# First norm of a two-block transformer kernel: squares summed in advance, root applied before the modulation, TensorE's first tiles reordered

## The reference, cut to what matters

```python
mod = c_act @ w_ada[layer] + b_ada[layer]            # c_act = silu(c), w_ada is 1024 x 6144
shift1, scale1, gate1, shift2, scale2, gate2 = jnp.split(mod, 6, axis=-1)
hn = x * rsqrt(mean(x * x) + EPS) * norm1_g
hn = hn * (1.0 + scale1) + shift1
proj = hn @ w_in[layer]
```

## Time and profile before

| what | value |
|---|---|
| runs of the kernel | 1587.87, 1588.24, 1588.24 us; median 1588.24 |
| the profiled execution, its own time | 1589.81 us |
| its span, first to last instruction | 1588.0 us |
| PE busy, share of the span | 1235.2 us, 78% |
| DVE busy | 451.4 us, 28% |
| ACT busy | 222.6 us, 14% |
| POOL busy | 150.9 us, 10% |
| moved by DMA | 542.93 MB, mean 342 GB/s |
| chain that ended last | PE 49%, DMA 40%, DVE 3%, ACT 1%, the rest smaller |
| mean granted clock of TensorE | 0.894 |

### The profile page before, as it was taken

The page is one execution under the profiler, slowest core; times in us unless marked ns, Lnnn a source line. Parts: engine busy times, 40 slices in busy tenths (PEclk is TensorE's granted clock), DMA queues, the critical chain, the costliest instruction groups (busy, mean ns, idle before and its releaser), DMA issues.

```text
span 1588.0 us, 17761 instructions
## 1 busy us (share of the span) xinstructions
PE 1235.2 (78%) x7570; PEld 691.3 (44%) x7570; DVE 451.4 (28%) x902; ACT 222.6 (14%) x458; POOL 150.9 (10%) x151
## 2 busy tenths in 40 slices
PE   7999999999999999987665566666566566656565
PEld 3876679998888888831111111111111111111111
DVE  4567756774533568220000000000000000000001
ACT  2324522232113231020000000000000000000001
POOL 1110056641100031000000000000000000000000
PEclk9999999999999999999787877787886887797878
DMA  9986476458944335799999999999999999999997
GB/s 387 342 264 248 168 291 213 160 175 335 394 155 159 106 114 209 296 364 429 428 428 429 428 428 429 428 428 428 428 429 428 428 428 429 428 428 429 427 429 304
DMA packets 52310, 542.93 MB, mean 342 GB/s; under 512 B 5932, under 2 KB 7980, under 8 KB 13196
## 3 DMA queue, kind: packets, MB, share of 16 engines
q1 hardware_dynamic: 45564, 511.03, 78.8%
q0 software_dynamic: 4352, 26.82, 4.3%
q10 hardware_dynamic: 2320, 3.98, 0.9%
HBM read 539.97 MB, written 1.84 MB: 341 GB/s over the span
## 4 chain that ended last, share of the span: by engine, by line
PE 49%; DMA 40%; another core or an unknown queue 4%; DVE 3%; ACT 1%; SPq 1%; issue 1%; ACTq 0%; DVEq 0%
DMA arena<-in_exp_w_dram 19%; DMA ring<-in_exp_w_dram 15%; PE L L1987 8%; PE L L2152 7%; DMA tok<-in_exp_w_dram 6%; PE X L2371 5%; PE L L2099 5%; PE X L2399 4%; PE L L1821 4%; PE X L2046 3%; PE L L1832 2%; PE L L2271 2%; PE L L1972 2%; PE X L2201 1%
## 5 line engine op out<-in xcount | busy, mean ns | idle before, releaser
L2371 PE MATMUL X<-arena,side 128*32 128x512 f32 x1280 | 194.6, 738 | 114.8 <-DMA arena<-in_exp_w_dram 114.8
L2371 PEld LDWEIGHTS X<-arena,side 128*32 128x32 f32 x1280 | 39.8, 123 | 268.5 <-DMA arena<-in_exp_w_dram 193.8
L1651 DVE TENSOR_TENSOR side<-side,X 128x512 f32<-128x512 f32 x16 | 11.0, 688 | 497.7 <-ACT side L998 497.7
L2371 PE MATMUL X<-ring,side 128*32 128x512 f32 x512 | 86.4, 808 | 71.1 <-DMA ring<-in_exp_w_dram 71.1
L2399 PE MATMUL X<-ring,side 128*32 128x512 f32 x512 | 81.4, 767 | 46.7 <-DMA ring<-in_exp_w_dram 46.4
L2152 PE MATMUL L<-tok,ring 128*128 128x256 f32 x448 | 99.4, 379 | 0.3 <-ACT tok L834 0.3
L665 POOL TENSOR_TENSOR side<-side 128x256 f32<-128x256 f32 x16 | 9.9, 616 | 869.5 <-DVE side L1661 806.7
L1656 DVE TENSOR_TENSOR side<-X,side 128x512 f32<-128x512 f32 x16 | 11.1, 692 | 281.5 <-PE X L2399 281.5
L2152 PEld LDWEIGHTS L<-tok,ring 128*128 128x128 f32 x448 | 84.3, 190 | 13.9 <-issue 3.1
L998 ACT ACTIVATE side<-X 128x512 f32<-128x512 f32 x16 | 9.6, 597 | 514.1 <-PE X L2371 514.1
L2099 PE MATMUL L<-arena,ring 128*128 128x256 f32 x352 | 77.4, 379 | 0.3 <-DVE arena L1391 0.3
(11 more groups left out here) (406 smaller groups left out, 1669.3 us busy)
## 6 DMA issues: line engine op xcount, KB each, us to landing
arena<-in_exp_w_dram SPq DMA_DIRECT2D x96, 2048.0 KB, 50.2
ring<-in_exp_w_dram SPq DMA_DIRECT2D x64, 2048.0 KB, 49.9
ring<-in_w_in_dram SPq DMA_DIRECT2D x34, 1024.0 KB, 5.2
more<-in_exp_w_dram SPq DMA_DIRECT2D x15, 2048.0 KB, 50.2
tok<-in_exp_w_dram SPq DMA_DIRECT2D x15, 2048.0 KB, 49.7
ring<-in_w_up_dram SPq DMA_DIRECT2D x22, 1024.0 KB, 4.9
ring<-in_w_ada_dram SPq DMA_DIRECT2D x16, 1024.0 KB, 9.5
arena<-in_ada_w_dram POOLq DMA_DIRECT2D x15, 1024.0 KB, 10.0
```

Source lines behind the costliest of these rows:

```text
L2371: last = MM(X[CAP * j:CAP * j + CAP, w, :], xe[:, k % 2, k // 2, :], v, start=(k == 0), stop=(k == KT - 1))
```

## The change

The squares of the first norm are summed by `norm_partial` and `sum_partial` too: `norm_partial` now stands ahead of `sine_arg(0)` on DVE. DVE multiplies `hT` by the root between `window(0)` and `window(4)`, before the modulation is known. Scale and shift are then one operation on each tile: even tiles on ACT, odd tiles on DVE. On PE, `mod_products(0)` to `mod_products(2)` stand between `sin1`, the sum, `rel` and `sin2`. The semaphore `sin_arg` is used a second time under the name `first_normed`.

```diff
--- before.py
+++ after.py
@@ -90,7 +90,7 @@
          "up_first": ("qk_sum", 2), "up_second": ("w3_done", 10), "up_third": ("scores_done", 16),
          "up_top": ("qk_inv", 2), "up_right": ("max_ready", 16), "up_corner": ("qk_ready", 8),
          "up_copied": ("qk_raw", 8), "ada2_landed": ("counts_landed", 16), "first0_landed": ("ctx_landed", 0), "first1_landed": ("router_landed", 0),
-         "first2_landed": ("masks_landed", 0), "first3_landed": ("dft_landed", 0), "first_summed": ("xT_done", 4)}
+         "first2_landed": ("masks_landed", 0), "first3_landed": ("dft_landed", 0), "first_summed": ("xT_done", 4), "first_normed": ("sin_arg", 2)}
 CHAIN_OF = {step: chain for chain, steps in CHAINS.items() for step in steps}
 
 
@@ -717,9 +717,10 @@
             A(rs[:, 2, :], rs[:, 1, :], ACT.Sqrt).then_inc(S["norm_root"], 1)
             sine(1)
             copy_mod_rows(0)
-            for k in range(KT):
-                act.wait_ge(S["norm_scaled"], k + 1)
-                A(hn[:, k, :], hn[:, k, :], ACT.Identity, bias=mod1[:, k:k + 1]).then_inc(S["norm_ready"], 1)
+            act.wait_ge(S["norm_scaled"], KT)
+            again(act, "first_normed", 1)
+            for k in range(0, KT, 2):
+                A(hn[:, k, :], hn[:, k, :], ACT.Identity, bias=mod1[:, k:k + 1], scale=gain[:, 0, k:k + 1]).then_inc(S["norm_ready"], 2)
 
             def filters_abs():
                 reached(act, "filt_windowed")
@@ -1027,12 +1028,23 @@
                 ins.then_inc(S[name], 1)
 
 
+            def norm_partial(kind, i):
+
+                if i in (1, 2):
+                    dve.wait_ge(S["norm_squares"], {"xT": 0, "wout": 4, "wdn": 8}[kind] + i + 1)
+                    last = V.tensor_tensor(hn[:, 0:2, :], hn[:, 0:2, :], hn[:, 2 * i:2 * i + 2, :], ALU.add)
+                    link(last)
+                if i == 2:
+                    done(V.tensor_tensor(hn[:, 0, :], hn[:, 0, :], hn[:, 1, :], ALU.add), "norm_partial")
+
             dve.wait_ge(S["cols_landed"], 16)
             dve.wait_ge(S["cond_ready"], 1)
             done(V.tensor_copy(cond1a, csil.unsqueeze(2).broadcast_to([P, KT, 32])), "cond_repeated")
             for i in range(4):
                 dve.wait_ge(S["xT_done"], i + 1)
                 done(V.tensor_copy(hT[:, 2 * i:2 * i + 2, :].rearrange("p a t -> p (a t)"), L[:, pos["xT"][i] % 4, :]), "lin_emptied_by_dve")
+            for i in (1, 2):
+                norm_partial("xT", i)
 
             def sine_arg(i):
 
@@ -1079,13 +1091,17 @@
             dve.wait_ge(S["rel_done"], 1)
             done(V.tensor_copy(t12[0:12, :], L[0:12, pos["rel"][0] % 4, :]), "lin_emptied_by_dve")
             window(0)
+            dve.wait_ge(S["norm_root"], 1)
+            for k in range(KT):
+                done(V.tensor_tensor(hn[:, k, :], hT[:, k, :], rs[:, 2, :], ALU.mult), "norm_scaled")
             window(4)
             dve.wait_ge(S["mod_cols_done"], 1)
             link(V.tensor_tensor(by_group(mod1[:, 0:16]), mod_cols(0, 0), by_group(colA[:, A_BADA:A_BADA + 16]), ALU.add))
-            link(V.scalar_tensor_tensor(gain[:, 0, :], mod1[:, 8:16], 1.0, colA[:, A_G1:A_G1 + 8], ALU.add, ALU.mult))
-            dve.wait_ge(S["norm_root"], 1)
-            for k in range(KT):
-                done(V.scalar_tensor_tensor(hn[:, k, :], hT[:, k, :], gain[:, 0, k:k + 1], rs[:, 2, :], ALU.mult, ALU.mult), "norm_scaled")
+            done(V.scalar_tensor_tensor(gain[:, 0, :], mod1[:, 8:16], 1.0, colA[:, A_G1:A_G1 + 8], ALU.add, ALU.mult), "first_normed")
+            again(dve, "first_normed", 1)
+            dve.wait_ge(S["norm_scaled"], KT)
+            for k in range(1, KT, 2):
+                done(V.tensor_scalar(hn[:, k, :], hn[:, k, :], gain[:, 0, k:k + 1], mod1[:, k:k + 1], ALU.mult, ALU.add), "first_normed")
 
 
             def invert_sums():
@@ -1282,15 +1298,6 @@
             reached(dve, "ctx_sum")
             link(V.tensor_scalar(rs[:, 0, :], X[:, 2, 0:T], 1.0 / D, EPS, ALU.mult, ALU.add))
             done(V.reciprocal(rs[:, 1, :], rs[:, 0, :]), "ctx_inv")
-
-            def norm_partial(kind, i):
-
-                if i in (1, 2):
-                    dve.wait_ge(S["norm_squares"], (4 if kind == "wout" else 8) + i + 1)
-                    last = V.tensor_tensor(hn[:, 0:2, :], hn[:, 0:2, :], hn[:, 2 * i:2 * i + 2, :], ALU.add)
-                    link(last)
-                if i == 2:
-                    done(V.tensor_tensor(hn[:, 0, :], hn[:, 0, :], hn[:, 1, :], ALU.add), "norm_partial")
 
             def residual(kind, gate):
 
@@ -1718,20 +1725,9 @@
             pe.wait_ge(S["x_landed"], 16)
             turn(xnat, "xT", "xT_done")
 
-            pe.wait_ge(S["sine_landed"], 16)
-            MM(aux("sin1")[0:64, 0:T], w1w, zw, start=True, stop=True).then_inc(S["sin1_done"], 1)
-
-            def sum_squares():
-
-                for k in range(KT):
-                    if k % 2 == 0:
-                        pe.wait_ge(S["norm_squares"], k // 2 + 1)
-                    last = MM(X[:, 0, 0:T], ones, hn[:, k, :], start=(k == 0), stop=(k == KT - 1))
-                last.then_inc(S["norm_sum"], 1)
-
             def sum_partial(n):
 
-                pe.wait_ge(S["norm_partial"], n)
+                pe.wait_ge(S["norm_partial"], n + 1)
                 pe.wait_ge(S["norm_squares"], 4 * n + 4)
                 for k in (0, KT - 2, KT - 1):
                     last = MM(X[:, 0, 0:T], ones, hn[:, k, :], start=(k == 0), stop=(k == KT - 1))
@@ -1744,7 +1740,10 @@
                 def tile(k):
                     if k not in waited:
                         waited.append(k)
-                        pe.wait_ge(S["norm_ready"], n * KT + k + 1)
+                        if n == 0 and k % 2:
+                            again(pe, "first_normed", k // 2 + 2)
+                        else:
+                            pe.wait_ge(S["norm_ready"], n * KT + k + (2 if n == 0 else 1))
                     return hn[:, k, :]
                 return tile
             def mod_products(m):
@@ -1848,13 +1847,17 @@
                     r = slice(32 * q, 32 * q + 32)
                     last = MM(X[:, q, :], each[r, :], hinv[n][r, :], start=True, stop=True)
                 last.then_inc(S["heads_spread"], 1)
-            sum_squares()
+            mod_products(0)
+            pe.wait_ge(S["sine_landed"], 16)
+            MM(aux("sin1")[0:64, 0:T], w1w, zw, start=True, stop=True).then_inc(S["sin1_done"], 1)
+            mod_products(1)
+            sum_partial(0)
             pe.wait_ge(S["small_landed"], 16 * 7)
             MM(aux("rel")[0:12, :], relw[0:32, :], ohw[0:32, :], start=True, stop=True).then_inc(S["rel_done"], 1)
-            mod_products(0)
+            mod_products(2)
             pe.wait_ge(S["sin_out"], 1)
             MM(aux("sin2")[:, 0:T], w2w, sint[0:64, 1, :], start=True, stop=True).then_inc(S["sin2_done"], 1)
-            for m in range(1, 8):
+            for m in range(3, 8):
                 mod_products(m)
                 if 4 <= m < 7:
                     third_layer((0, 2, 4)[m - 4], (2, 2, 4)[m - 4])
```

## The result

The changed kernel takes 1594.15 us (median of 6 runs, 1589.94 to 1594.76) against 1588.05 for the kernel before in the same comparison (6 runs, 1586.71 to 1589.28). The ratio is 1.0033, with a 95% interval of 1.0022 to 1.0043. It is slower by a third of a per cent, outside the range that was given.

What follows compares the result with a forecast made beforehand. PE's long run, starting at 39.09 us and reached through DVE, was taken as the bound. Product 7 2.4 us earlier, less 1.5 for root products, plus 0.5 from the joined operation, gave 1.4: 1588.24 becomes 1586.8, range 1585.0 to 1589.9.

Steps and rivals of the forecast that it cites:

- The chain and its propagation: Moving the start of PE's long run at 39.09 us moves the whole time equally; nothing later absorbs the shift.
- Pre-adds, landings, third layer: Early on PE: pre-adds end at 14.5 us, slot 4 lands at 23.2, third layer starts at 24.15, 2.4 us earlier.
- The early root and the joined operation: Before the long run: eight root products on DVE add 1.5 us to the path; joined scale and shift saves 0.5.
- rival B: TensorE's clock falls in PE's new gaps, costing 3 us, so 1.6 us slower than before: 1589.8 us; chance 0.12.
- The baseline: Sum made on the profiled execution, 1589.81 us, 1.57 above the median; 1588.4 and 1588.24 less 1.4 gives 1586.8.
- Rival A: Head start mostly lost through a late clock rise and dearer root products: about 1588.0 us; chance 0.20 together with Rival D.
- Rival C: Root products before window(4) fit wholly into DVE's waiting, saving 1.5 us more: 1585.4 us; chance 0.11.
- Rival D: Slot landings set the start, so cutting PE's sum gains nothing: 1588.2 us; chance 0.20 together with Rival A.

Runs made afterwards that it cites:

- e3: Changed kernel with 23 fillers instead of 8 behind the turned modulation columns, 12 ahead of product 3 and 6 ahead of product 4; 1587.88 us, ratio 0.9997.
- e7: Changed kernel with PE's old order, the eight-product sum, no pre-adds, and 23 fillers at the tail; 1588.95 us, ratio 1.0002.
- e1: The changed kernel, unaltered, run again for a second trace; 1594.96 us, ratio 1.0037, traced execution 1595.54 us.
- e5: Changed kernel with 12 fillers ahead of product 3 and 6 ahead of product 4, none added at the tail; 1589.06 us, ratio 1.0003.
- e9: The kernel before, unaltered, a single execution for a second trace; 1587.33 us.
- e10: The kernel before, unaltered, a single execution for a third trace; 1587.58 us.
- e12: e3 with two memsets behind the odd tiles' scaling, the root products ahead of window(0), and 10 tail fillers instead of 23; 1586.27 us, ratio 0.9988.
- e11: The kernel before with 10 filler transposes in PE's pause from 10.5 to 12.95 us; 1587.18 us, ratio 0.9993.
- e6: Changed kernel with PE's old order, the three-product sum kept, and 23 fillers at the tail; 1589.79 us, ratio 1.0006.

## Why the prediction was wrong

The forecast was 1586.8 us and "the same"; measured were 1594.15 and slower by 0.33%. Point by point, by its own steps:

- **The chain and its propagation** were right. The run's start decides, nothing behind it absorbs a shift, and in none of the traces is a DMA among what PE waits for between the run's start and 715 us. The constant, 1548.2 to 1550.0 us over all fourteen traces, shows it over a range of starts from 36.0 to 44.3.
- **Pre-adds, landings, third layer** were right within 0.2 us where the clock was high. In e3 the pre-added sum, products 3 and 4 behind their slots, the third layer at 24.32 (forecast 24.15), and the long run at 37.50 (forecast 37.7) are close to the prediction's own timetable.
- **The early root and the joined operation**: I put 1.5 us on the path less 0.5, 1.0 lost in all; e7 has 0.96 less 0.33, 0.63 lost. Both terms have the right sign, the first is 0.5 too large and the second 0.2 too large (the column scale that I cost at nothing took 0.09 us). That e3's start comes within 0.2 us of 37.7 is therefore partly luck.
- **The step that failed** is rival B's place and price. I saw that between 19.05 and 23.2 only product 3 is work, gave the fall of the clock 0.12, and priced it at 3 us from the 6 us that PE had needed to become fast in the earlier trace rows. It fell in both traces of the changed kernel. Ten of its eleven runs took 1593.0 to 1595.5 us, and the medians of e1 and e5 put the price at 5.9 us (5.4 by the ratios). In e1 PE was slow from 20.6 to 40 us, not for six, and its long run began 6.6 us behind the forecast 37.7. The price came from one stretch of work and was applied to another; why the clock came back so much later there was not tested.
- **The range** had no case for it. I let the fall of the clock end after a time known from elsewhere in the trace, when the only bound from above was the end of the stretch: from 20.7 to 31.9 some 10 us of work, which could take twice as long. To a slowdown of over 0.2% I gave 0.04, on the ground that the clock would have to be lost twice; in e1 it was lost once.
- **The baseline** was also wrong. The sum was made against one traced execution whose own time lay 1.57 us above the median. I carried that difference over to the changed kernel as if it were a fixed offset. It was the very thing at stake: in e9 and e10 the clock was high for more of the start, and the run began 1.8 and 1.9 us earlier. Against those, a start of 37.5 gains nothing, which is what e3 shows (ratio 0.9997). The gain of 1.4 us was a gain on an unlucky execution.
- **The other rivals.** Rival A's number, 1588.0, is where e3 came out (1587.88), for the reason just given and not for its own. Rival C's waiting lay at another place (e12). Rival D, that landings govern, holds once the clock is high: in e3, with six records in the sum, the third layer starts at 24.32, 1.0 us after slot 4 lets product 4 start; in e11, with all sixteen, it starts at 24.00, again 1.0 us after product 4. Cutting the sum brought nothing there.

Why the clock stayed low in ten runs of eleven, and only briefly in the first traced one, is settled only so far: where the wait ahead of product 3 is filled or the order is the old one, none of 33 runs (e3, e5, e6) is near 1594. What decides whether it returns before 24.8 us (first trace) or at 40 (e1) is open.

## What to carry to other kernels

When work is cut or moved ahead of transfers, look at what PE does in the time that comes free: a wait of 1.75 us for a weight slot cost some 6 us through the clock, and 18 short transposes, whose results nobody reads, took it back. What such a fall costs depends on where it comes: ahead of the long run a wait of 2.1 to 2.4 us cost 1.7 us. As the upper bound take all the work between the gap and the next long run at half speed, not the shortest recovery that the trace shows. And when a profiled execution lies above the median of its kernel, find out what it lost before making a sum against it; and put an extra operation where its engine waits, which is not always where its input first exists.

## What the runs showed of the hardware

The granted clock of the windows can hide a slow stretch. In the trace of before it reads 1.00 between 15 and 17 us:

```profile
15.00:17.00 2.00, 2.00 (x6) 1.64 (x5) 1.86 (x7) 0.02 (x1) 0.00 (x0) 1.00 1.04 424
```

while the sum's records there took 634 ns, against 379 at full speed. In e9 the same stretch shows it:

```profile
13.00:15.00 2.00, 2.00 (x8) 1.49 (x7) 1.52 (x4) 0.20 (x1) 0.00 (x0) 0.76 1.02 422
15.00:17.00 2.00, 2.00 (x7) 1.55 (x6) 1.42 (x8) 0.73 (x2) 0.00 (x0) 0.50 0.99 408
17.00:19.00 2.00, 2.00 (x8) 1.20 (x7) 0.29 (x1) 0.97 (x1) 0.00 (x0) 0.88 1.03 424
```

In the rows compared here the reading was wrong only ahead of the first fall that it showed. It is 1.00 from 7 us on in every trace, while the transposes there take about 420 ns each, against 273 for the same shape in the fillers of e3's tail; in e6 it is 1.00 from 14 to 25 us while the sum's records take 634 ns and product 0 takes 1.94 us. So durations of like records are the safer reading. The Trainium skill, "TensorE: Matmul & The Clock Gate", Part 1, "Seeing it yourself", warns that the clock's events in a trace have been seen to be unreliable; these rows agree.

The e9 rows also show that the clock was high at first behind the pause of 2.05 us (sin1 took 0.64 us) and fell afterwards, while PE worked: a gap's price can come a microsecond or two after the gap. In the trace of before sin1 took 1.11 us and the clock had not yet risen, as the prediction read it. The same kernel has both histories, and they set the start of its long run 1.8 us apart.

The full clock did not return for 17 us of gapless PE work in e1 (23.10 to 39.83), where in e6 it was back within 13 us of the last gap (14.42 to 27.44) and in the first trace of the changed kernel within 4 us of the gap (20.85 to 24.78). The Trainium skill, "TensorE: Matmul & The Clock Gate", Part 1, "What's actually happening", says that activity releases the half rate. These rows agree, and show that the release can come far later than the trace of before alone suggests.
